# A two-block transformer kernel on one core: DVE sums the weighted input blocks of modulation chunks before PE multiplies them

## The reference

```python
silu_c = jax.nn.silu(c)                    # (1, 1024)
for i in range(DEPTH):                     # DEPTH = 2
    mod = silu_c @ ada_w[i] + ada_b[i]     # (1, 1024) @ (1024, 6144)
    sh1, sc1, g1, sh2, sc2, g2 = split(mod, 6)
    h = rms_norm(x, norm_mix_g[i]) * (1.0 + sc1) + sh1
    y = diff_attention(h, ...)  or  chunked_attention(h, ...)
    x = x + g1 * y
    h = rms_norm(x, norm_ffn_g[i]) * (1.0 + sc2) + sh2
    x = x + g2 * grouped_moe(h, ...)
# the third layer: silu(c_2) and silu(c_ctx_2), each @ w_mod_2 (1024, 6144)
```

## Time and profile before

| | us |
|---|---|
| median of three runs | 1631.85 |
| the profiled execution, whole | 1637.57 |
| its span in the trace | 1635.8 |
| PE busy | 1581.2 |
| DVE busy | 505.6 |
| ACT busy | 396.2 |
| POOL busy | 52.0 |

### The profile page before, as it was taken

How to read it: one execution, slowest core, us unless ns; L and a number is a source line. 1 busy time by engine, 2 the same in 40 slices (tenths; PEclk the granted TensorE clock), 3 DMA queues, 4 the chain that set the end, 5 groups by cost and what they waited for, 6 DMA issues and landing times.

```text
span 1635.8 us, 21483 instructions
## 1 busy us (share of the span) xinstructions
PE 1581.2 (97%) x8665; PEld 901.9 (55%) x8665; DVE 505.6 (31%) x1259; ACT 396.2 (24%) x861; POOL 52.0 (3%) x65
## 2 busy tenths in 40 slices
PE   6999989999999999999999999889999999999998
PEld 3665665444456747644545876557644545454444
DVE  2043432323231242431222255433332222323122
ACT  1142321111131432411211253342311212111121
POOL 0000010000000001000000034001000000000000
PEclk9999989999999999899999999789899999999999
DMA  9998749999998777599999400430599999999995
GB/s 355 341 340 305 307 205 425 428 428 429 428 368 297 262 285 307 216 425 427 429 429 417 176 1 1 159 151 0 238 423 429 430 427 428 429 428 428 429 428 228
DMA packets 94819, 535.21 MB, mean 327 GB/s; under 512 B 7951, under 2 KB 11881, under 8 KB 70194
## 3 DMA queue, kind: packets, MB, share of 16 engines
q1 hardware_dynamic: 94354, 534.36, 80.2%
q10 hardware_dynamic: 416, 0.17, 0.0%
HBM read 533.45 MB, written 1.06 MB: 327 GB/s over the span
## 4 chain that ended last, share of the span: by engine, by line
PE 87%; DMA 8%; ACT 1%; DVE 1%; SPq 1%; issue 1%; POOL 0%; DVEq 0%; POOLq 0%; ACTq 0%
PE pair L1000 26%; PE bank L987 7%; PE pair L1007 6%; PE bank L1007 6%; PE bank L731 6%; DMA ring<-in_w_dram 4%; PE bank L1049 3%; PE bank L627 3%; PE pair L1049 3%; PE pair L1077 3%; PE bank L825 2%; PE bank L738 2%; PE pair L707 2%; DMA arena<-in_b_s_dram 1%; PE bank L1077 1%; DMA ring<-in_a_w_qkv_dram 1%
## 5 line engine op out<-in xcount | busy, mean ns | idle before, releaser
L1000 PE MATMUL pair<-ring,arena 128*64 128x512 f32 x2048 | 447.3, 594 | 0.6 <-DMA ring<-in_w_dram 0.6
L1000 PEld LDWEIGHTS pair<-ring,arena 128*64 128x64 f32 x2048 | 144.5, 137 | 285.2 <-issue 284.8
L2307 DVE TENSOR_TENSOR arena<-sq,pair 128x512 f32<-128x512 f32 x32 | 33.9, 1061 | 387.2 <-PE pair L1000 387.2
L987 PE MATMUL bank<-arena 128*128 128x128 f32 x1120 | 139.8, 280 | 3.2 <-DVE arena L2189 3.2
L987 PEld LDWEIGHTS bank<-arena 128*128 128x128 f32 x1120 | 134.0, 196 | 3.5 <-issue 3.4
L1007 PE MATMUL pair<-ring,arena 128*64 128x512 f32 x512 | 116.9, 598 | 0.0
L731 PE MATMUL bank<-hh,ring 128*128 128x256 f32 x512 | 115.1, 382 | 1.1 <-DMA ring<-in_a_w_qkv_dram 1.1
L1007 PE MATMUL bank<-ring,arena 128*64 128x512 f32 x512 | 115.3, 592 | 0.0
L1682 ACT ACTIVATE sq<-pair 128x512 f32<-128x512 f32 x32 | 19.1, 597 | 366.2 <-PE pair L1000 366.2
L731 PEld LDWEIGHTS bank<-hh,ring 128*128 128x128 f32 x512 | 95.8, 190 | 21.1 <-issue 8.4
L2286 DVE TENSOR_SCALAR arena<-bank,affine_rows 128x128 f32<-128x128 f32 x140 | 47.8, 404 | 103.2 <-PE bank L987 103.2
(11 more groups left out here) (403 smaller groups left out, 1655.0 us busy)
## 6 DMA issues: line engine op xcount, KB each, us to landing
ring<-in_w_dram SPq DMA_DIRECT2D x96, 2048.0 KB, 15.5
ring<-in_moe_w_gate_dram SPq DMA_DIRECT2D x32, 2048.0 KB, 11.7
ring<-in_moe_w_up_dram SPq DMA_DIRECT2D x32, 2048.0 KB, 16.4
ring<-in_moe_w_down_dram SPq DMA_DIRECT2D x32, 2048.0 KB, 14.2
ring<-in_ada_w_dram SPq DMA_DIRECT2D x24, 2048.0 KB, 16.9
ring<-in_w_mod_dram SPq DMA_DIRECT2D x12, 2048.0 KB, 11.1
ring<-in_a_w_qkv_dram SPq DMA_DIRECT2D x6, 2048.0 KB, 20.2
ring<-in_b_w_qkv_dram SPq DMA_DIRECT2D x6, 2048.0 KB, 16.2
```

What stands on the lines that cost most here:

```text
L987: last = mm(b[part][:, cols(k % 4)], h_tok[:, t, cols(k)], pick_n[:, t, :], start=(t == 0), stop=(t == TT - 1))
L1000: last = mm(b[2 + m][half(a), :], x_sel[:, k, half(a)], R8[moe_slot(l, a, m)][:, k, :], start=(k == 0), stop=(k == KT - 1))
L2307: tt(hid.rearrange("p (f q) -> p q f", f=FT), by_row(gate_act), by_row(b[3]), ALU.mult).then_inc(M["hid_ready"], 1)
```

## The change

A table `PRODUCTS` names 27 chunks. For 23 of them PE multiplies only blocks 0, 1 and 2 by silu(c) itself, and for four (4, 5, 20 and 21) none. The blocks left, five or eight of them, are summed by DVE in `weighted_rows(g)`: the first is scaled in its place in the ring slot by its silu(c) column, then each further block is multiplied by its own column and added to it. Every step is an instruction over 128 x 512 numbers, and each but the last waits for its end. PE then multiplies the sum in one matmul by a window of a new table `C_WIN` (one column of ones), and waits for it by `csil_ready`. So PE issues four matmuls for 23 chunks and one for four chunks, in place of eight. Chunks 0 to 3, 10 and 24 to 27 stay as they were.

On DVE the sums stand at fixed places: A0 to A3 ahead of `head_scale(10)`; in layer 0, A4 ahead of `normed(0, 0)`, A5 ahead of `normed(1, 0)` and A7 ahead of `head_scale(19)`; B0 ahead of `mods_add`; B1 and B2 behind `normed(1, 1)`; B3 between `maxima(4)` and `maxima(5)`; B4, B5 and B6 behind `half_out(0)`, `(1)` and `(2)`; B7 behind `weights(7)`.

```diff
--- before.py
+++ after.py
@@ -64,7 +64,8 @@
 C_SPR = C_DUP + 256
 C_ROW = C_SPR + 256
 C_OCT = C_ROW + 128
-N_CST = C_OCT + KT
+C_WIN = C_OCT + KT
+N_CST = C_WIN + 63
 C2_SPREAD = 0
 N_CST2 = 4 * P
 
@@ -86,6 +87,7 @@
     c[::32, C_ROW:C_ROW + P] = 1.0
     c[p, C_OCT + p // 16] = 1.0
     c[p, C_PICK + p % 32] = 1.0
+    c[:, C_WIN + 31] = 1.0
     c[:, C_IOTA:C_IOTA + 64] = np.arange(64)
     t = np.arange(S)
     inv = (1.0 / (np.float32(10000.0) ** (np.arange(0, 32, 2, dtype=np.float32) / np.float32(32)))).astype(np.float32)
@@ -540,6 +542,24 @@
                 return csil, i
             return csil2, 4 + 2 * n if batch == 4 else 2 * i
 
+        PRODUCTS = {4: 0, 5: 0, 6: 3, 7: 3, 8: 3, 9: 3, 11: 3, 12: 3, 13: 3, 14: 3, 15: 3, 16: 3, 17: 3, 18: 3, 19: 3,
+                    20: 0, 21: 0, 22: 3, 23: 3, 28: 3, 29: 3, 30: 3, 31: 3, 32: 3, 33: 3, 34: 3, 35: 3}
+        summed_at = lambda g: 3 + list(PRODUCTS).index(g)
+
+        def mod_products(g):
+
+            n = PRODUCTS.get(g, KT)
+            parts = [(k, k % 4) for k in range(n)]
+            return parts if n == KT else parts + [(n, g % 4 if n == 0 else 3)]
+
+        def quarter_ends(batch, last):
+
+            seen = {}
+            for g in (reversed(batch) if last else batch):
+                for k, q in (reversed(mod_products(g)) if last else mod_products(g)):
+                    seen.setdefault(q, (g, k))
+            return set(seen.values())
+
         reverse = lambda a: a.rearrange("p (t i) -> p t i", t=TT)[:, :, ::-1]
         blocks = lambda a: a.rearrange("p (t i) -> p t i", t=TT)
         at_q = lambda qt: slice(0, P) if qt == 0 else slice(P, P + S)
@@ -617,15 +637,20 @@
             def mods(g):
 
                 batch = next(i for i, r in enumerate(BATCHES) if g in r)
-                first, last_g = BATCHES[batch][0], BATCHES[batch][-1]
+                first = BATCHES[batch][0]
                 if g == first and batch >= 1:
                     pe.wait_ge(mod_ready, batch)
                 w = chunk_in(mod_at[g])
                 c_, r = mod_window(g)
-                for k in range(KT):
-                    q = slice(k % 4 * 32, k % 4 * 32 + 32)
-                    last = mm(b[7][q, :], c_[:, k, 31 - r:63 - r], w[:, k, :], start=(g == first and k < 4),
-                              stop=(g == last_g and k >= KT - 4))
+                opens, closes = quarter_ends(BATCHES[batch], False), quarter_ends(BATCHES[batch], True)
+                for k, q in mod_products(g):
+                    row = c_[:, k, 31 - r:63 - r]
+                    if k == PRODUCTS.get(g, KT):
+                        if summed_at(g) == 3:
+                            pe.wait_ge(table_in, 16)
+                        pe.wait_ge(csil_ready, summed_at(g))
+                        row = K(C_WIN + 31 - r, 32)
+                    last = mm(b[7][32 * q:32 * q + 32, :], row, w[:, k, :], start=((g, k) in opens), stop=((g, k) in closes))
                 last.then_inc(mod_rows, 1)
 
             def mods_turn(batch):
@@ -1937,6 +1962,17 @@
                 ins.then_inc(dve_step, 1)
                 dve.wait_ge(dve_step, steps[0])
 
+            def weighted_rows(g):
+
+                n, first = mod_at[g], PRODUCTS[g]
+                dve.wait_ge(full[slot_of_chunk(n)], 16 * (n // NSLOT + 1))
+                w, (c_, _) = R8[slot_of_chunk(n)], mod_window(g)
+                total = w[:, first, :]
+                then(ts(total, total, c_[:, first, 31:32], None, ALU.mult))
+                for k in range(first + 1, KT - 1):
+                    then(stt(total, w[:, k, :], c_[:, k, 31:32], total, ALU.mult, ALU.add))
+                stt(total, w[:, KT - 1, :], c_[:, KT - 1, 31:32], total, ALU.mult, ALU.add).then_inc(csil_ready, 1)
+
             def eight_copies():
                 return nc.vector.tensor_copy(eight_ids.rearrange("p (a q) -> p a q", a=KT),
                                              ident.unsqueeze(1).broadcast_to([P, KT, P]))
@@ -2100,8 +2136,15 @@
                     stt(xT[:, c, :], b[c % 2][:, 0:S], mod[:, l, G1 + c:G1 + c + 1], xT[:, c, :],
                         ALU.mult, ALU.add).then_inc(x_half, 1)
 
+                A, B = BATCHES[2 * l + 2], BATCHES[2 * l + 3]
+                for g in A[:4]:
+                    weighted_rows(g)
                 head_scale(10)
+                if l == 0:
+                    weighted_rows(A[4])
                 normed(0, 0)
+                if l == 0:
+                    weighted_rows(A[5])
                 normed(1, 0)
                 dve.wait_ge(bias_in, 16 * (l + 1))
                 then(nc.vector.memset(bias[HEAD:P, 0:8 * (l + 1), P + 64:S], NEG))
@@ -2113,25 +2156,35 @@
                 maxima(3)
                 weights(2)
                 weights(3)
+                if l == 0:
+                    weighted_rows(A[7])
                 head_scale(19)
                 if l == 0:
                     out_scale(0)
+                weighted_rows(B[0])
                 mods_add(2 * l + 2)
                 normed(0, 1)
                 normed(1, 1)
+                weighted_rows(B[1])
+                weighted_rows(B[2])
                 if l == 0:
                     out_normed(0)
                 maxima(4)
+                weighted_rows(B[3])
                 maxima(5)
                 weights(4)
                 half_out(0)
+                weighted_rows(B[4])
                 maxima(6)
                 weights(5)
                 half_out(1)
+                weighted_rows(B[5])
                 maxima(7)
                 weights(6)
                 half_out(2)
+                weighted_rows(B[6])
                 weights(7)
+                weighted_rows(B[7])
                 half_out(3)
                 half_out(4)
                 half_out(5)
```

## The result

The changed kernel took 1650.88 us, the median of five runs from 1644.01 to 1652.97, where it had been 1631.85. The ratio is 1.0096, 95% interval 1.0075 to 1.0118, so 12 to 19 us slower. The forecast was 1646 in 1636 to 1658.

The account below looks back on a forecast made before the run. PE looked full, but DVE's ordered list was to become the bound in the B stretches. Layer 0 11.3 us late, layer 1 1.7, clock 1.0: 14.0 us on the median 1631.85 gives 1646, range 1636 to 1658.

Parts of the forecast that it names:

- What bounds the stretch: Attention of both layers: PE is full, and DVE is free for only 10.5 of 25 us and 20 of 35.
- Price of a sum: On DVE: about 750 ns per multiply-and-add, so 3.6 us for five blocks, 5.9 for eight, 106 us for all 27.
- The worst row, 1432 ns: Upper bound for one multiply-and-add on a ring slot, seen where POOL works; it would give over 1660 and was left out.
- double-rate rival: DVE's multiply-and-add runs at 483 ns like the scaling, a sum takes 2.5 us, total 1633; chance 0.10.
- What PE saves: On PE: 0.92 us per four-matmul chunk, 2.5 us per pair with one matmul each, 26 us over the kernel.
- A chunks, layer 0: Before scores(0): A4 and A5 delay it, a load holds PE anyway, and the projection behind it starts 1 us late.
- B0 to B2: Layer 0: sums of B1 and B2 (7.2 us) delay out_normed(0), so scores(4) starts 1.2 us late.
- B3 to B7: Layer 0, largest term: DVE's list from maxima(4) to the last sum takes 34.3 us; the layer ends 11.3 us late.
- Layer 1: Scores(0) 3.4 us early, scores(4) at 589.8 instead of 594.34, then DVE's 32.3 us list; 1.7 us late at the end.
- Clock: PE's waits for sums bring clock drops, mostly in time PE has to spare; 0.5 us for each layer.
- the rival in which the clock falls for good: PE's waits hold its clock at the lower level through both lists, 7.5 us per layer, total 1660; chance 0.12.
- the rival in which every sum is hidden: PE stays the bound and gains 21 us of its 26, total 1611; chance 0.05.

Follow-up runs that it names:

- e4_dve_alone: Changed kernel, layer 0 only: PE does eight matmuls per chunk, waiting for no sum; DVE runs the same steps on a constant table; ratio 1.0107 to the kernel before.
- e3_one_step: Changed kernel with DVE doing only the first step of each of the 27 sums, other blocks left out of the product; ratio 0.9962 to the kernel before.
- e5_layer0: Changed kernel with the change in layer 0 alone (15 sums), layer 1 as before; ratio 1.0084 to the kernel before.
- e7_no_a4_a5: Changed kernel without the sums of A4 and A5 of layer 0 (chunks 8 and 9); ratio 1.0090 to the kernel before.
- e8_one_step_late: Changed kernel with one step for each sum and chunks 4 to 9 as eight matmuls again; ratio 0.9965 to the kernel before.

## Why the prediction was right, point by point

- *What bounds the stretch.* Right. DVE's free time in the B stretches was the number to read, not its 31%. With the 18 us of sums in 10.5 free, DVE is at 22.37 of 25 us and PE drops to 19.01. e4_dve_alone shows that DVE's time alone makes the loss of layer 0; e3_one_step, that without it there is none.
- *Price of a sum.* I took 3.6 us from 748 ns a step; a step measured 752 ns, and the sum from 168.80 to 172.34 is 3.54 us. The worst row, 1432 ns, played no part, with POOL at 0.00. The Trainium skill's rule ("VectorE: DVE Perf Modes", "Why `tensor_tensor` can't do 2×_2P or 4×") agrees with this trace: 752 ns for two tensors, 480 for the scaling with one. The double-rate rival is out.
- *What PE saves.* 0.9 us for a chunk with four matmuls is right where the sum is there in time. Chunks 20 and 21 together pass in 0.98 us (514.07 to 515.05), I took 1.1. But where PE has to wait for the sum, a chunk falls into two rounds, 1.06 us for the three products and 1.05 for the sum alone (B7 of layer 0), against 1.92 before: nothing is saved. I had forecast 0.6 us for a last matmul. Eleven chunks waited, and this is one reason why PE's busy time fell by 8 us and not by 26; e3_one_step, with almost no such waits, has 1563.1 us, 18 less than before.
- *A chunks, layer 0.* 1 us late was forecast for the projection behind scores(0). Where the clock did not fall it was 0.6: it starts 45.3 us after the layer's origin in e5_layer0 (96.09), 44.6 in e7_no_a4_a5 without the two sums, 44.7 before. In the profile after it was 1.6, behind scores(0) at the lower clock (1.65 us in place of 0.93).
- *B0 to B2.* Scores(4) was to be 1.2 us late, waiting for out_normed. It does wait for it, 1.69 us (L2094), and is 1.7 late in the layer's own time in the profile after, 0.7 in e5_layer0.
- *B3 to B7.* I had 34.3 us for DVE's list; in the trace it runs from 158.18 to 193.6, 35.4 us. Most of the difference is two waits of DVE, 0.99 and 0.80 us, for an output projection of PE that took 2.68 and 3.35 us in place of 1.99. Layer 0 was forecast 11.3 us late: e5_layer0 gives 11.4, the profile after 13.4. That 11.4 comes so near is in part luck: 0.7 up to scores(4) and 10.7 from there, where 1.2 and 10.1 were forecast.
- *Layer 1.* It was to be early by 3.4 at scores(0) and 4.5 at scores(4), late by 1.7 at the end; measured 3.44, 4.47 and 1.6.
- *Clock.* This is the mis-sized term. I put 0.5 us in each layer. The profile after has a granted clock of 0.86 in 160 to 185 us and about 2 us of layer 0 on it; layer 1 has 1.00 and nothing, with waits of up to 2.7 us in it, so the rival in which the clock falls for good is out. The clock differs between executions of the same layer (0.93 in e5_layer0), so a profile's own total can't be trusted to 5 us here. Two slips of the prediction changed nothing in its sum. A granted clock of 0.89 over 15 us is 3.3 us at the lower level, as I wrote, but that is 22% of the stretch and not 11%. And 5.76 us was the longest head of PE before; the next two took 4.76 us (171.57 to 176.33 to 181.09), so at the lower clock these would need 7.7 us with the change, against 7.8 of DVE, and that rival's 7.5 us was too much for layer 0.
- *The most that could be gained.* I gave 21 us to the rival in which every sum is hidden. No run came near it: e3_one_step and e8_one_step_late have nearly free sums and gain 6 us. I had counted the load only for the A chunks of layer 0, and wrote that for B3 to B7 of layer 0 the loads don't enter. That holds for the change, where DVE is later than they are; once DVE's time is gone, the chain through a load of 21.3 us ends both layers. Besides the loads PE of e3_one_step waits for DVE more than before: 5.2 us against 0.7 in 60 to 205 us, most of it for the reciprocal, normed and out_normed.

What stays open: the medians lie 19 us apart and the stretches account for 15 less 1.3 (the wait behind the router shrank from 3.54 to 2.32 us). The interval, 12 to 19 us, holds both, and no run tells the rest from chance.

## What to carry to other kernels

Before moving work to an engine that looks idle, read its busy time in the very stretch where the work will stand, and write its ordered list there, with the old entries; if the list is longer than the other engine's, the move lengthens the stretch by the difference, however little the average says. Work is worth moving where its new engine is idle and where nothing on that engine is waited for behind it: the eight of these 27 sums that meet this and shorten something turn 16 us of loss into 5 of gain (1.0096 and 0.9969). Then ask whether a load would have held the relieved engine anyway; here, in the kernel with the sums all but free, a load stood at the end of both layers.

## What the runs showed of the hardware that I had not expected

A wait of PE of 2.50 us ahead of a projection was followed by 0.50 of the granted clock (1.2 GHz) and cost 2.8 us; a wait of 2.73 us at the same place in another kernel was followed by no drop at all, and the projection took its 3.69 us. In the profile after, waits of no more than 1.75 us came ahead of a drop (0.57 in 88 to 96 us), and the same waits in e5_layer0 did not bring one. One such wait therefore predicts neither a drop nor its absence.
